# Delta rule on raw keys and queries, with the next head's products handed out in single matmuls

## The chip, the core and the metric

One core of one Trainium2 chip runs the whole program once. The metric is device microseconds for that run. The program computes two small model blocks in float32; the change touches one of their mixers, the chunked gated delta rule with 8 heads.

## The reference, cut to what matters

```python
qkv = silu(causal_depthwise_conv(h @ w_in[qkv]))          # 4 taps, 512 tokens
q = l2norm(q) * 128 ** -0.5                               # l2norm(x) = x * rsqrt(sum(x * x) + EPS)
k = l2norm(k)
beta, g = sigmoid(b_in), -exp(a_log) * softplus(a_in + dt_bias)
# per head, chunks of C tokens, g_cum = cumsum(g) in the chunk, decay = exp(g_cum_i - g_cum_j), j <= i
kb = k * beta
L = where(strict, (kb @ k.T) * decay, 0);  A = L + I
u, w = solve(A, v * beta), solve(A, kb * exp(g_cum))
attn = (q @ k.T) * decay
for each chunk:                                           # state S is 128 x 128
    v_new = u - w @ S
    o = (q * exp(g_cum)) @ S + attn @ v_new
    S = S * exp(g_last) + (k * exp(g_last - g_cum)).T @ v_new
y = (rmsnorm(o, norm_g) * silu(gate)) @ w_out             # rmsnorm divides by sqrt(mean(o * o) + EPS)
```

## The kernel before, in words

Activations lie transposed: channels on 128 partitions, 512 tokens along a row. A head is one tile of 128 channels; its tokens are handled as TT = 4 chunks of 128, each with two blocks of 64 for the triangular inverse. The program is written out engine by engine; each engine runs its own list in order and waits on semaphores.

**Dense products.** TensorE computes the four projections of a head (key, query, value, gate: "slabs" j = 0 to 3) from weights split into a high and a low part, 8 slices of 128 rows by 3 matmuls of 512 columns each: 24 matmuls per slab, 96 per head (lines L618 to L620). They are for head i + 1 and are put between the small products of head i by `fill(first, end)`, in groups of one slice (3 matmuls) to two slices and more. GpSimd splits each slab with two instructions (`split`, L555 high part, L557 low part, both read and write SBUF). `split(s)` waits for `slab_done` of slab s - 3, so a slab's last matmul starts the split of the third slab after it.

**Small products of head i on TensorE,** in order: keys by keys-times-beta into B3 (L911, wait `kb`), keys by queries into B4 (L919, wait `qn`), transposes of the keys into B7 (L643), a transposition of the first inverse (L892, wait `xt`), five levels of the inverse (L892: a group into banks 0 and 1 that waits for `x`, then after a fill two groups `xq` and `xp`), two last steps (L943, L949), w (L957), and for each chunk L964 (u), L968 (minus w by state, waits for `s`), L971 (state by queries), a fill, L975 (state update) and L976 (output). Then `head_squares` (L824: two matmuls by ones, for the squared norms of keys and queries), `head_rows` (L833: decay and beta rows broadcast over partitions), and L983, a matmul by ones of the squared output.

**VectorE** runs the convolution taps of head i + 1 (L2215), the masks and subtractions of the inverse (L2299, L2304, L2308), the state (L2331, L2334), scaled copies of transposed keys and values (`kv_scaled`, L2272), and at the end of a head `ada_rows(i)` (three products with a reduction of 128x1024, L2000, for another part of the program) and `head_start(i + 1)` (L2224 to L2232). The next head begins with L2248 (B3 times decay), four masked copies L2253 and L2256, which releases `xt`. `head_end` (L2237, L2239) makes the gated output of the head before.

**ScalarE** holds the activations, among them `head_rnorms` (log and exp of the norms over 128x512), the exponent of the decay, table loads (Silu set, Ln/Exp set), and copies of PSUM banks.

Of the kernel before, what the change touches and what calls it, by code (L numbers as in the profile page):

```python
# [24 lines left out]
P = 128  # L25
# [137 lines left out]
def build(nc, a, out):  # L163
    ctx = ExitStack()
    with ctx:
# [33 lines left out]
        vraw, osq, ors, head_out = yt[:], A[:, 11], A[:, 10], A[:, 11]  # L199
# [29 lines left out]
        S = sb("S", [P, 2, P])  # L229
        mx, nm, esum, rinv = sb("mx", [P, 2]), sb("nm", [P, 2]), sb("esum", [P, 2]), sb("rinv", [P, 2])  # L230
# [57 lines left out]
        def r_slab(i, j):  # L288
# [25 lines left out]
        tr_ready, pt_ready, pv_done = sem("tr_ready"), sem("pt_ready"), sem("pv_done")  # L314
# [13 lines left out]
            "ab_in", "ab_hi", "ab_lo", "ab_ps", "abT", "ab", "gates", "gsum", "pick", "rowhi", "rowlo", "row", "silu", "sq", "ss", "rn", "rows", "kb", "qn", "dec", "erow", "gram", "ktr",  # L328
# [18 lines left out]
        def half_block(t, tile, b):  # L347

            return t[HALF * b:HALF * b + HALF, tile * HALF:(tile + 1) * HALF]

# [230 lines left out]
        def _(pe):  # L581

            pe.sem_inc(tr_ready, 2)
            pe.sem_inc(pv_done, 2)
# [226 lines left out]
            q, k_, v, gs0, E, dec, gs1, LT, kdec, XT, ktok, wT, Pm, vn = (A[:, n] for n in range(14))  # L811
            gs, attn = (gs0, gs1), dec

            def head_sums(i, chunks):

                for pair in range(2):
                    pair_chunks(SLAB0["gdn"] + i * 4 + 2 * pair, USE0["gdn"] // 2 + i * 2 + pair,
                                [c - 2 * KD * pair for c in chunks if c // (2 * KD) == pair])
# [7 lines left out]
            def head_rows(i):  # L826

                if i:
                    pe.wait_ge(g["s"], i * 3)
                else:  # L830
                    pe.wait_ge(g["rowlo"], 2)
                for n, bank in enumerate((SS, B5)):
                    mm = pe.matmul(bank[:], pick[0:64, i:i + 1].broadcast_to((64, P)), gate_row[:, n, :], start=True, stop=True)  # L833
                mm.then_inc(g["rows"], 1)

            def out_step(name, n, k, ready):

                s, u = SLAB0[name], USE0[name] // 2
                if n == 0:
# [4 lines left out]
                for j in range(2):  # L844
# [28 lines left out]

            def head(i, ahead):

                def fill(first, end, step=None, kv=None, third=()):
                    if ahead:
                        head_sums(i + 1, range(first, end))
                    elif kv is not None:
                        kv_slabs(f"kv{kv // 2}", (kv % 2,))  # L880
                    elif step is not None:
                        out_step("gdn_out", step, step, step + 1)
                    if not ahead:
                        for k in third:
                            out_third("gdn_out", k, k, k + 1)

                def blocks(out, lhs, left, rhs, right, take, put, bs=(0, 1)):

                    for t in range(TT):
                        for b in bs:  # L890
                            at = b ^ (t % 2 & take)
                            mm = pe.matmul(out(t, b ^ (t % 2 & put)), left(lhs, t, at), right(rhs, t, at), start=True, stop=True)  # L892
                    return mm

                def first_two(t, b):
                    return pair_block(0, t, b)

                def next_two(t, b):
                    return pair_block(2, t, b)

                def last_one(t, b):
                    return half_block(B5, t, b)

                def on_ident(rhs, t, b):
                    return rhs[HALF * b:HALF * b + HALF, HALF * b:HALF * b + HALF]

                fill(0, 5, kv=0)
# [5 lines left out]
                fill(5, 7, kv=1)  # L913
                pe.wait_ge(g["qn"], i + 1)
# [6 lines left out]
                turn_over(B7, [k_[:, t * P:(t + 1) * P] for t in range(TT)]).then_inc(g["ktr"], 1)  # L921
                fill(7, 8, kv=2)
# [4 lines left out]
                fill(8, 10, kv=3)  # L927
                for n in range(1, 6):
                    pe.wait_ge(g["x"], i * 6 + n)
                    blocks(first_two, LT, own_block, Xs, half_block, 0, 1).then_inc(g["p_ps"], 1)  # L930
                    fill(8 + 2 * n, 10 + 2 * n, n - 1)
                    if n == 1 and i:
                        pe.wait_ge(yt_ready, i)
# [4 lines left out]
                    if n == 2:  # L938
                        turn_over(B7, [vraw[:, t * P:(t + 1) * P] for t in range(TT)]).then_inc(g["vtr"], 1)

# [4 lines left out]
                fill(20, 22, 5)  # L945
# [5 lines left out]
                fill(22, 24)  # L951

                pe.wait_ge(g["tok"], i + 1)
# [5 lines left out]

                pe.wait_ge(g["v"], i + 1)  # L960
                pe.wait_ge(g["qd"], i + 1)
                for t in range(TT):
                    c = slice(t * P, (t + 1) * P)
                    mm = pe.matmul(B4[:, c], XT[:, c], v[:, c], start=True, stop=t == 0)  # L964
# [7 lines left out]
                    fill(24 + t, 25 + t)  # L972
# [4 lines left out]
                mm.then_inc(g["o_ps"], 1)  # L977
                if ahead:
                    head_squares(i + 1)
                    head_rows(i + 1)  # L980
                fill(28, 30, third=(0, 1))
                pe.wait_ge(g["osq"], i + 1)
                pe.matmul(B4[:], ones, osq, start=True, stop=True).then_inc(g["oss"], 1)  # L983
                fill(30, 32, 6, third=(2, 3, 4))

            head_sums(0, range(KD, KD + 2))
            gates_of_tokens()
            head_sums(0, range(KD + 2, 2 * KD + 3))
            gate_sums()
            head_sums(0, range(2 * KD + 3, 4 * KD))  # L990
            head_squares(0)
            head_rows(0)
# [3 lines left out]
            out_step("gdn_out", 7, 7, 8)  # L996
            for k in range(5, KD):
                out_third("gdn_out", k, k, k + 1)
            out_rest("gdn_out")
# [429 lines left out]
        def _(act):  # L1429
# [181 lines left out]
            q, k_, v, gs0, E, dec, gs1, LT, kdec, XT, ktok, wT, Pm, vn = (A[:, n] for n in range(14))  # L1611
            gs, attn = (gs0, gs1), dec

            def head_sum(i, j):
# [3 lines left out]
                if i:  # L1618
                    act.wait_ge(*((g["ktr"], i), (g["qd"], i), (g["vtr"], i))[j])
# [7 lines left out]
            def head_square(i, j):  # L1627

                act.wait_ge(g["silu"], i * 3 + j + 1)
                act.activation(sq[:, j, :], (k_, q)[j], ACT.Square).then_inc(g["sq"], 1)  # L1630

            def head_rnorms(i):

                for j, (bank, times) in enumerate(((B3, 1.0), (B7, P ** -0.5))):
                    inv_sqrt(g["ss"], i * 2 + j + 1, tb[:, j, :], bank[:], 1.0, times, load=False).then_inc(g["rn"], 1)

            def head_gate(i):

                copy_sum(1, SLAB0["gdn"] + i * 4 + 3, gs[i % 2])

            def head_start(i):

                head_rnorms(i)
                act.wait_ge(g["dec"], i + 1)
                act.activation(dec, dec, ACT.Exp).then_inc(g["edec"], 1)
                act.activation(E, SS[:], ACT.Exp).then_inc(g["erow"], 1)

            def head_end(i):
                inv_sqrt(g["oss"], i + 1, ors, B4[:], 1.0 / P, load=False).then_inc(g["ors"], 1)
                if i == 6:  # L1650

                    act.wait_ge(g["qn"], 8)
                    kv_copies(0)
                act.wait_ge(yt_ready, i + 1)
                high_y(i, i, head_out)

            def head(i, ahead):
                if ahead:
                    head_sum(i + 1, 0)
                    head_sum(i + 1, 1)  # L1660
                act.preload_act_table_set(SILU)
                if not ahead:
                    kv_copies(1)
                act.wait_ge(taken[1], USE0["gdn"] // 2 + i * 2 + 3)
                act.activation(gs[i % 2], gs[i % 2], ACT.Silu).then_inc(g["gs"], 1)
                if ahead:
                    head_silu(i + 1, 0)
                act.wait_ge(g["wt_ps"], i + 1)
                act.activation(wT, B3[:], ACT.Copy, scale=-1.0).then_inc(g["wt"], 1)
                for t in range(TT):  # L1670
# [3 lines left out]
                    if ahead:  # L1674
# [3 lines left out]
                        elif t == 1:  # L1678
# [1120 lines left out]
```

## Time and profile before

| | |
|---|---|
| median of 3 runs | 2233.44 us (2232.42 to 2235.02) |
| profiled execution, first to last instruction | 2231.0 us |
| TensorE busy | 2160.1 us, 97% |
| VectorE, ScalarE, GpSimd busy | 1170.1, 574.0, 1215.7 us |
| mean granted TensorE clock | 0.994 of full speed |

The profiled execution stands 2.4 us under the median, which also counts what lies around the instructions. A busy share tells that an engine had work in flight. What limits a stretch is read from the timeline of each engine: which instruction starts late, and what released it. The delta rule takes the stretch from about 94 us to 469 us.

### The profile page before, as it was taken

Reading aid. Unit: us, or ns where it says so; the run is one execution under the profiler, and the core shown is the slowest. Engines: PE = TensorE matmul, PEld = TensorE weight load, DVE = VectorE, ACT = ScalarE, POOL = GpSimd, SP = SyncE. Lnnn points to the kernel's source line nnn. Section 1 sums busy time; section 2 is a strip of 40 time slices with the busy share of each in tenths; the row PEclk is TensorE's granted clock in tenths of the full one; section 3 lists DMA queues with packets and bytes.
Section 4 is the critical chain, followed back from the end, with each engine's and each line's share of the span. In section 5 each row is a group of like instructions: output and inputs, shape, how many; then the busy total and the mean of one; then the engine's idle time right before and its main releaser. Section 6 shows DMA issues by size and latency. Waiting matters only on the chain.

```text
span 2231.0 us, 29287 instructions
## 1 busy us (share of the span) xinstructions
PE 2160.1 (97%) x11992; PEld 1724.0 (77%) x11992; DVE 1170.1 (52%) x1651; ACT 574.0 (26%) x1043; POOL 1215.7 (54%) x687
## 2 busy tenths in 40 slices
PE   7899999999999999999999999999999999999998
PEld 6677777778888887677788888777777778887886
DVE  4666666658648275554431322467765365346332
ACT  4333423223112022342320201422232230002113
POOL 5433233357868676433566666654436276656663
PEclk9999999999999999999999999999999999999999
DMA  8522322236556453211333333322224133333331
GB/s 271 181 68 80 101 67 86 86 103 206 164 180 198 152 188 109 68 51 39 113 97 101 96 94 96 100 79 67 66 57 128 43 110 98 95 95 94 105 104 66
DMA packets 366018, 239.88 MB, mean 108 GB/s; under 512 B 11351, under 2 KB 350653, under 8 KB 365758
## 3 DMA queue, kind: packets, MB, share of 16 engines
q1 hardware_dynamic: 364268, 234.07, 35.0%
q10 hardware_dynamic: 1618, 3.94, 0.5%
q8 instruction: 96, 1.57, 0.3%
q14 instruction: 36, 0.29, 0.0%
HBM read 233.79 MB, written 4.19 MB: 107 GB/s over the span
## 4 chain that ended last, share of the span: by engine, by line
PE 88%; DVE 6%; ACT 2%; issue 1%; POOL 1%; DMA 1%; SPq 0%; DVEq 0%; ACTq 0%; POOLq 0%
PE bank L599 16%; PE bank L601 16%; PE bank L600 16%; PE bank L618 6%; PE bank L620 5%; PE bank L619 5%; PE mid L892 2%; PE mid L1355 1%; PE bank L635 1%; PE bank L637 1%; PE bank L636 1%; PE bank L846 1%; POOL wL L557 1%; PE mid L643 1%; PE bank L848 1%
## 5 line engine op out<-in xcount | busy, mean ns | idle before, releaser
L555 POOL TENSOR_SCALAR wH<-stage 128x1024 fp32r<-128x1024 f32 (+1 forms) x340 | 386.0, 1135 | 960.1 <-PE bank L620 370.6
L557 POOL TENSOR_TENSOR wL<-stage,wH 128x1024 fp32r<-128x1024 f32 (+1 forms) x340 | 830.5, 2443 | 28.4
L599 PE MATMUL bank<-hH,wH 128*128 128x512 f32 x944 | 368.6, 390 | 0.7 <-DVE A L2077 0.3
L601 PE MATMUL bank<-hH,wL 128*128 128x512 f32 x944 | 367.4, 389 | 0.0
L600 PE MATMUL bank<-hL,wH 128*128 128x512 f32 x944 | 367.3, 389 | 0.0
L599 PE MATMUL bank<-RA,wH 128*128 128x512 f32 (+1 forms) x788 | 283.9, 360 | 5.5 <-DVE RA L2091 3.0
L601 PE MATMUL bank<-RA,wL 128*128 128x512 f32 (+1 forms) x788 | 281.7, 358 | 0.0
L600 PE MATMUL bank<-RA,wH 128*128 128x512 f32 (+1 forms) x788 | 281.6, 357 | 0.0
L618 PE MATMUL bank<-hH,wH 128*128 128x512 f32 x544 | 239.4, 440 | 6.5 <-POOL wL L557 6.2
L620 PE MATMUL bank<-hH,wL 128*128 128x512 f32 x544 | 214.1, 394 | 0.0
L619 PE MATMUL bank<-hL,wH 128*128 128x512 f32 x544 | 213.4, 392 | 0.0
L599 PEld LDWEIGHTS bank<-hH,wH 128*128 128x128 f32 x944 | 177.2, 188 | 39.8 <-issue 3.3
L600 PEld LDWEIGHTS bank<-hL,wH 128*128 128x128 f32 x944 | 177.2, 188 | 36.8 <-issue 0.2
L601 PEld LDWEIGHTS bank<-hH,wL 128*128 128x128 f32 x944 | 177.2, 188 | 36.8
L599 PEld LDWEIGHTS bank<-RA,wH 128*128 128x128 f32 x788 | 149.3, 189 | 29.5 <-DVE RA L2091 3.2
L600 PEld LDWEIGHTS bank<-RA,wH 128*128 128x128 f32 x788 | 149.4, 190 | 21.6 <-issue 0.5
L601 PEld LDWEIGHTS bank<-RA,wL 128*128 128x128 f32 x788 | 149.3, 190 | 21.4
L1508 ACT ACTIVATE A<-bank 128x512 f32<-128x512 f32 (+1 forms) x85 | 47.2, 558 | 384.1 <-PE bank L601 354.6
L2000 DVE CUSTOM_DVE_ANT_0 WIDE<-WIDE,cbc,vec 128x1024 f32<-128x1024 f32 x80 | 142.9, 1831 | 0.1
L2060 DVE SCALAR_TENSOR_TENSOR xT<-bank,modT,xT 128x512 f32<-128x512 f32 x62 | 46.4, 750 | 172.8 <-PE bank L601 164.6
L2129 DVE TENSOR_TENSOR A<-bank,A 128x512 f32<-128x512 f32 x44 | 30.5, 692 | 197.4 <-PE bank L601 191.8
L618 PEld LDWEIGHTS bank<-hH,wH 128*128 128x128 f32 x544 | 102.6, 189 | 39.3 <-issue 12.6
(406 smaller groups left out, 3232.7 us busy)
## 6 DMA issues: line engine op xcount, KB each, us to landing
WIDE<-in_ada_t SPq DMA_DIRECT2D x46, 1024.0 KB, 6.0
stage<-in_ffn_w_gate SPq DMA_DIRECT2D x44, 512.0 KB, 3.8
stage<-in_ffn_w_up SPq DMA_DIRECT2D x44, 512.0 KB, 3.8
stage<-in_c_wkv SPq DMA_DIRECT2D x32, 512.0 KB, 3.9
stage<-in_gdn_w_in SPq DMA_DIRECT2D x32, 512.0 KB, 4.0
stage<-in_ffn_w_down SPq DMA_DIRECT2D x32, 512.0 KB, 3.8
stage<-in_o_w_in SPq DMA_DIRECT2D x32, 512.0 KB, 4.0
stage<-in_e_w_in SPq DMA_DIRECT2D x26, 512.0 KB, 3.7
```

Source lines behind the costliest of these rows:

```text
L555: pool.tensor_scalar(high[:, 0:n], raw[:, 0:n], 1.0, 0.0, ALU.mult, ALU.add).then_inc(w_high, 1)
L557: pool.tensor_tensor(low[:, 0:n], raw[:, 0:n], high[:, 0:n].bitcast(F32), ALU.subtract).then_inc(w_split, 1)
L599: pe.matmul(bank[:, 0:n], h[:, k, c], xh[:, k, :], start=first and k == 0, stop=False)
L600: pe.matmul(bank[:, 0:n], h[:, k, c], xl[:, k, :], start=False, stop=False)
L601: mm = pe.matmul(bank[:, 0:n], l[:, k, c], xh[:, k, :], start=False, stop=last and k == kc - 1)
L618: pe.matmul(acc[j % 2][:], h, hH[:, k, :], start=k == 0, stop=False)
L619: pe.matmul(acc[j % 2][:], h, hL[:, k, :], start=False, stop=False)
L620: mm = pe.matmul(acc[j % 2][:], l, hH[:, k, :], start=False, stop=k == KD - 1)
L892: mm = pe.matmul(out(t, b ^ (t % 2 & put)), left(lhs, t, at), right(rhs, t, at), start=True, stop=True)
L1508: act.activation(out, acc[b][:, 0:n], func).then_inc(taken[b], 1)
L2000: ins = dve.tensor_tensor_reduce(out=w, in0=w, in1=c_bank if n < ADA_HEAD else cbc[:], scale=1.0, scalar=vec[:, at:at + 1], op0=ALU.mult, ...
L2060: dve.scalar_tensor_tensor(out=xT[:, k, :], in0=bank[:], scalar=gate[:, k:k + 1], in1=xT[:, k, :], op0=ALU.mult, op1=ALU.add).then_inc(tak ...
```

## The change

Keys and queries are no longer normalised over 128x512. The norm of a key becomes a factor per token, taken from squares of the transposed keys (`key_squares`, sums over 128x128 tiles into `k_sum`) and put into the bias of the decay's exponent, into `kdec_by` and into `v_by`. The norm of the query goes into the output norm (`head_sums`). The two matmuls by ones of L824 and the mask `strict` are gone; scaled copies move from VectorE to ScalarE in four tiles each; the dense products are counted in single matmuls (`head_units`) and spread in more and smaller groups. Cut to its core:

```diff
-        vraw, osq, ors, head_out = yt[:], A[:, 11], A[:, 10], A[:, 11]
+        vraw, osq, ors, head_out = yt[:], A[:, 17], A[:, 16], A[:, 17]
...
@@ TensorE
-            def head_squares(i):
-                for j, bank in enumerate((B3, B7)):
-                    pe.wait_ge(g["sq"], i * 2 + j + 1)
-                    pe.matmul(bank[:], ones, sq[:, j, :], start=True, stop=True).then_inc(g["ss"], 1)
+            def head_squares(i):
+                pe.wait_ge(g["osum"], i + 1)
+                pe.matmul(B4[:], ones, osq, start=True, stop=True).then_inc(g["oss"], 1)
...
-                fill(0, 5, kv=0)
+                at = dense(9)
+                if not ahead:
+                    kv_slabs("kv0", (0,))
+                if i:
+                    head_squares(i - 1)
+                at = dense(3)
                 pe.wait_ge(g["kb"], i + 1)
...
-                fill(5, 7, kv=1)
-                pe.wait_ge(g["qn"], i + 1)
+                at = dense(9)
...
-                turn_over(B7, [k_[:, t * P:(t + 1) * P] for t in range(TT)]).then_inc(g["ktr"], 1)
-                fill(7, 8, kv=2)
+                at = dense(3)
                 pe.wait_ge(g["xt"], i * 7 + 1)
...
-                fill(8, 10, kv=3)
+                at = dense(6)
                 for n in range(1, 6):
                     pe.wait_ge(g["x"], i * 6 + n)
                     blocks(first_two, LT, own_block, Xs, half_block, 0, 1).then_inc(g["p_ps"], 1)
-                    fill(8 + 2 * n, 10 + 2 * n, n - 1)
+                    at = dense(3)
...
                     blocks(last_one, Ps, half_block, XTs, half_block, 1, 1).then_inc(g["xp"], 1)
+                    at = dense(3)
...
-                fill(20, 22, 5)
+                at = dense(3)
...
-                fill(22, 24)
+                at = dense(6)
...
                 for t in range(TT):
+                    elif ahead:
+                        keys_turn(i + 1)
-                    fill(24 + t, 25 + t)
+                    at = dense(4)
                     pe.wait_ge(g["vn"], i * 4 + t + 1)
...
+                    at = dense(2)
+                    if ahead and t == 1:
+                        head_rows(i + 1, 0)
+                    if ahead and t == TT - 1:
+                        head_rows(i + 1, 1)
+                at = dense(3)
...
@@ ScalarE
+            def head_open(i):
+                if i:
+                    head_squares(i - 1)
+                act.preload_act_table_set(LN_EXP)
+                own.settle()
+                act.activation(k_log, k_sum, ACT.Ln, bias=EPS).then_inc(g["rk"], 1)
+                act.wait_ge(g["rk"], 3 * i + 1)
+                act.activation(k_inv2, k_log, ACT.Exp, scale=-1.0).then_inc(g["rk"], 1)
+                act.activation(k_norm, k_log, ACT.Exp, scale=0.5).then_inc(g["rk"], 1)
+                act.wait_ge(g["dec"], i + 1)
+                act.wait_ge(g["kds"], 3 * i + 1)
+                for t in range(TT):
+                    ins = act.activation(decs[i % 2][:, c], decs[i % 2][:, c], ACT.Exp, bias=dec_bias[:, t:t + 1])
+                ins.then_inc(g["edec"], 1)
...
@@ VectorE
-            def head_start(i):
...
+            def key_factors(i):
+                dve.wait_ge(g["rk"], 3 * i + 1)
+                dve.scalar_tensor_tensor(out=dec_bias, in0=k_log, scalar=-1.0, in1=tok[:, 0, :, i],
+                                         op0=ALU.mult, op1=ALU.subtract).then_inc(g["kds"], 1)
+                dve.wait_ge(g["rk"], 3 * i + 3)
+                dve.tensor_tensor(kdec_by, k_inv2, tok[:, 3, :, i], ALU.mult).then_inc(g["kds"], 1)
+                dve.tensor_tensor(v_by, k_norm, tok[:, 1, :, i], ALU.mult).then_inc(g["kds"], 1)
+            def head_sums(i):
+                dve.wait_ge(g["osq"], i + 1)
+                dve.wait_ge(g["sq"], i + 1)
+                dve.scalar_tensor_tensor(out=osq, in0=sq[:, i % 2, :], scalar=Q_EPS, in1=osq,
+                                         op0=ALU.mult, op1=ALU.add).then_inc(g["osum"], 1)
...
-                ada_rows(i)
-                if ahead:
-                    head_start(i + 1)
+                if ahead:
+                    decay_rows(i + 1)
+                    keys_by_beta(i + 1)
+                head_sums(i)
+                if ahead:
+                    key_factors(i + 1)
+                ada_rows(i)
```

`decay_rows` adds the table `decay_neg` to SS (PSUM) in one 128x512 instruction; `keys_by_beta` multiplies B5 (PSUM) by the keys. The gated output of head i - 1 (`head_scaled`, `head_gated`) now reads a copy `vn` of B6 that ScalarE makes. `between(n)` of VectorE now holds at n = 1 `head_scaled`, n = 2 `head_gated`, n = 3 E times q, n = 4 `low_y`, n = 5 a tap of the query; `below(n)` the key's three taps at n = 1 to 3 and a query tap at n = 4.

## Rows read from the trace of the kernel before

**Rows 1.** Page, busy time of the engines, with share of the span and instructions.
```profile
PE 2160.1 (97%) x11992; PEld 1724.0 (77%) x11992; DVE 1170.1 (52%) x1651; ACT 574.0 (26%) x1043; POOL 1215.7 (54%) x687
```
**Rows 2.** Busy time by stretch: start:end length, PE, PEld, DVE, ACT, POOL, PEclk, DMA share, GB/s.
```profile
270.40:315.60 45.20, 43.80 (x436) 33.12 (x435) 30.21 (x63) 15.46 (x28) 14.04 (x8) 1.00 0.30 94
```
**Rows 3.** Timeline of PE: start, length, line, tiles, count; end of one head, start of next.
```profile
270.43 0.38 PE L976 MATMUL mid<-A 128*128 128x128 f32 x2
270.65 1.02 PE L824 MATMUL mid<-sq,tab 128*128 128x512 f32 x2
...
272.46 0.72 PE L833 MATMUL mid<-RA,pick 64*128 64x512 f32 x2
...
273.45 0.40 PE L619 MATMUL bank<-hL,wH 128*128 128x512 f32 x1
273.69 0.40 PE L620 MATMUL bank<-hH,wL 128*128 128x512 f32 x1
...
284.66 0.46 PE L892 MATMUL mid<-tab,inv 64*64 64x64 f32 x16
```
**Rows 4.** Timeline of PE, one level of the inverse in the same head.
```profile
288.84 0.46 PE L892 MATMUL mid<-A,inv 64*64 64x64 f32 x16
289.12 0.63 PE L892 MATMUL mid<-inv,A 64*64 64x64 f32 x16
289.92 0.46 PE L892 MATMUL mid<-inv,A 64*64 64x64 f32 x16 [0.16 <-DVE inv L2304]
...
290.64 0.40 PE L619 MATMUL bank<-hL,wH 128*128 128x512 f32 x1
```
**Rows 5.** Timeline of PE, last step of the inverse and the chunks of that head.
```profile
305.16 0.68 PE L949 MATMUL mid<-A 64*64 64x64 f32 x8 [0.41 <-DVE A L2319]
...
310.13 0.46 PE L968 MATMUL mid<-S,A 128*128 128x128 f32 x2
...
311.34 0.38 PE L975 MATMUL mid<-A 128*128 128x128 f32 x2
...
312.25 0.46 PE L968 MATMUL mid<-S,A 128*128 128x128 f32 x2
...
315.59 0.38 PE L976 MATMUL mid<-A 128*128 128x128 f32 x2
```
**Rows 6.** Timeline of DVE around the start of that head.
```profile
269.65 1.27 DVE L2000 CUSTOM_DVE_ANT_0 WIDE<-WIDE,cbc,vec 128x1024 f32<-128x1024 f32 x1
...
273.26 1.12 DVE L2224 SCALAR_TENSOR_TENSOR A<-mid,tok,tab 128x128 f32<-128x128 f32 x4
...
281.43 0.69 DVE L2248 TENSOR_TENSOR A<-mid,A 128x512 f32<-128x512 f32 x1 [5.13 <-PE mid L911]
282.16 1.24 DVE L2253 TENSOR_TENSOR inv<-A,tab 64x128 f32<-64x128 f32 x4
283.43 0.42 DVE L2256 TENSOR_TENSOR inv<-tab,inv 128x256 f32<-128x256 f32 x1
...
284.38 0.16 DVE L2259 COPY chunk_decay<-A 128x4 f32<-128x4 f32 x1
```
**Rows 7.** Timeline of ACT, end of that head.
```profile
315.70 1.28 ACT L1684 ACT_TABLE_LOAD   x1
```
**Rows 8.** Timeline of POOL in that head.
```profile
277.18 1.05 POOL L555 TENSOR_SCALAR wH<-stage 128x1024 fp32r<-128x1024 f32 x1 [11.26 <-PE bank L620]
...
284.89 1.05 POOL L555 TENSOR_SCALAR wH<-stage 128x1024 fp32r<-128x1024 f32 x1 [4.19 <-PE bank L620]
```
**Rows 9.** Timeline of DVE in the last head.
```profile
417.47 3.35 DVE L2253 TENSOR_TENSOR inv<-A,tab 64x128 f32<-64x128 f32 x4
...
422.66 2.35 DVE L2259 COPY chunk_decay<-A 128x4 f32<-128x4 f32 x1
```
**Rows 10.** Timeline of POOL in the last head.
```profile
417.65 2.39 POOL L557 TENSOR_TENSOR wL<-stage,wH 128x1024 fp32r<-128x1024 f32 x1
```
**Rows 11.** Timeline of PE in the last head, a wait.
```profile
429.43 0.47 PE L846 MATMUL bank<-RA,wH 128*128 128x512 f32 x1 [1.87 <-ACT tb L1508]
```
**Rows 12.** Busy time by stretch, as in rows 2, shortly after that wait.
```profile
430.20:433.50 3.30, 3.30 (x52) 2.51 (x50) 0.62 (x2) 0.00 (x0) 2.14 (x1) 0.50 0.51 145
```

More of the change, by code:

```diff
@@ L826, in head_rows @@
-            def head_rows(i):
-                if i:
[L829 to L836, printed above, removed]
+            q, k_, v, gs0, E, dec0, gs1, LT, kdec, XT, ktok, wT, Pm, vn = (A[:, n] for n in range(14))
@@ new lines, in _, with head_units @@
+            gs, attns = (gs0, gs1), (dec0, A[:, 14])
+            def head_units(i, first, end):
+                for n in range(first, end):
+                    j, k, part = n // (3 * KD), n // 3 % KD, n % 3
+                    s, uses = SLAB0["gdn"] + i * 4 + j, USE0["gdn"] // 2 + i * 2 + j // 2
+                    if k == 0 and part == 0:
+                        pe.wait_ge(w_split, s + 1)
+                        free(j % 2, uses)
+                    h, l = (w[:, k, :] for w in halves(s))
+                    mm = pe.matmul(acc[j % 2][:], l if part == 2 else h, (hL if part == 1 else hH)[:, k, :],
+                                   start=k == 0 and part == 0, stop=k == KD - 1 and part == 2)
+                    if k == KD - 1 and part == 2:
+                        mm.then_inc(slab_done, 1)
@@ new lines, in head_rows, with keys_turn @@
+            def head_rows(i, n):
+                if i == 0:
+                    pe.wait_ge(g["rowlo"], 2)
+                elif n == 0:
+                    pe.wait_ge(g["p"], i * 6)
+                else:
+                    pe.wait_ge(g["s"], i * 3)
+                pe.matmul((SS, B5)[n][:], pick[0:64, i:i + 1].broadcast_to((64, P)), gate_row[:, n, :],
+                          start=True, stop=True).then_inc(g["rows"], 1)
+            def keys_turn(i):
+                pe.wait_ge(g["silu"], i * 3 + 1)
+                if i:
+                    pe.wait_ge(g["v"], i)
+                turn_over(B7, [k_[:, t * P:(t + 1) * P] for t in range(TT)]).then_inc(g["ktr"], 1)
@@ L843, in out_step @@
                 pe.wait_ge(y_ready, ready)
-                for j in range(2):
+                for j in js:
                     h, l = (w[:, k, :] for w in halves(s + j))
@@ L872, in out_rest, with blocks, first_two, next_two @@
                             behind(k)
+            def blocks(out, lhs, left, rhs, right, take, put, bs=(0, 1)):
+                for t in range(TT):
+                    for b in bs:
+                        at = b ^ (t % 2 & take)
+                        mm = pe.matmul(out(t, b ^ (t % 2 & put)), left(lhs, t, at), right(rhs, t, at), start=True, stop=True)
+                return mm
+            def first_two(t, b):
+                return pair_block(0, t, b)
+            def next_two(t, b):
+                return pair_block(2, t, b)
@@ L877, in fill @@
                     if ahead:
[L878 to L893, printed above, removed]
@@ L2386, in _ @@
             conv(0, 2, (2, 1, 0))
-            head_start(0)
+            decay_rows(0)
+            keys_by_beta(0)
+            key_factors(0)
             for i in range(0, 7):
```

282 lines of the change are left out of this document (147 added, 135 removed).

## The prediction

> **What bounds the kernel now.** I read the engines' busy time first: TensorE is busy 97% of the span [rows 1], so a change counts only by what it does to TensorE's list. Next, the table by stretch over one head: TensorE has 43.80 us of work in 45.20, at the full clock (1.00, that is 2.4 GHz), VectorE 30.21, GpSimd 14.04 in 8 instructions [rows 2]. Seven heads repeat this. I call T the start of the last chunk's output product L976; T is 270.43 for one head and 315.59 for the next, so a head takes 45.16 us [rows 3, 5]. Then the timelines of TensorE, VectorE and GpSimd side by side: who would be late if TensorE came sooner? In the kernel before nobody is: VectorE's three long products run from T - 0.8 to T + 2.8, GpSimd's splits start at T + 6.8 and T + 14.5, and VectorE, which waited 5.13 us, starts L2248 at T + 11.0 [rows 6, 8]. That order is what the change moves.
>
> **TensorE's own list, per head.** Dense matmuls start 0.23 apart [rows 3].
> - Gone: the two matmuls by ones, from 270.65 to 272.46: -1.8 [rows 3].
> - Chunks: from a state update L975 to the next use of the state L968 it is 0.91 us [rows 5], while three products lie between at 0.22 each (L976 takes 0.22 to the next start [rows 3]): 0.25 is waiting, thrice. Two dense matmuls now stand there and hide it: -0.75, and at most as much again because the first product after a wait starts cold; I take -1.0.
> - Before L949 0.41 of waiting [rows 5] is covered by the dense group that follows more closely: -0.4.
> - Levels of the inverse: from the second group after a fill (289.12) to the next level's first (289.92) it takes 0.80, of which some 0.35 waits for VectorE [rows 4]: the first group of 16 needed 0.28, and this one is 0.17 longer (0.63 against 0.46). Three dense matmuls now stand in that gap. But a group of 64x64 products costs to enter and to leave: from 289.92 to the second dense matmul at 290.64 it takes 0.72, 0.2 more than 0.28 + 0.23 [rows 4]; entering costs another 0.1. So 0.35 is won and 0.3 paid, five times: -0.3, between -1.8 (the switch is free) and +1.5 (the wait stays).
> - The row products (L833) are split over two places, one more switch: +0.3, between 0 and 0.6. The key transposes only move.
> Sum: -1.8 - 1.0 - 0.4 - 0.3 + 0.3 = -3.2; the smaller waits at the first transposition and the first chunk bring it to -3.6. If nothing else were late a head would take 41.6.
>
> By the Trainium skill, "TensorEngine Tiling (Array Packing)", changing the tiling mode drains TensorE. The 0.2 and 0.1 above agree with it; it speaks against the smaller groups, and without it the levels would give -1.8 instead of -0.3.
>
> **Work that moves to ScalarE** (tile copies, squares of 128x128) lies beside 45 us of TensorE work with 15.46 busy [rows 2]; I cost it at nothing, at most 0.5 a head where a copy sits behind another. No row shows a square with a sum; the chunk copies are its neighbours.
>
> **Where VectorE now comes late.** TensorE reaches the wait for `xt` sooner: before at T + 14.2 (284.66) with 36 dense matmuls in between [rows 3]; now 29 (2, 12, 3, 9, 3), without the ones products, one row product and the key transposes: 14.2 - 1.6 - 1.8 - 0.3 - 0.45 = about 10.2. But VectorE's three L2000 (269.65 to 273.26, 3.6 us [rows 6]) now stand behind `keys_by_beta`, `head_sums` and `key_factors`. `keys_by_beta` waits for the second row product, issued after the last chunk, so it runs from T + 1.4 to 2.0; `head_sums` to T + 2.7. `key_factors` waits for a logarithm that stands behind a table load of 1.28 [rows 7], after the squared output that waits for L976: T + 2.6. That would still do: 2.7 + 0.2 + 3.6 = 6.5, then L2248 0.73, L2253 1.27, L2256 0.4: `xt` at T + 9.
>
> The splits break it. The gate slab of the next head is now finished three matmuls after the second row product: its split starts at T + 2.4 instead of T + 6.8 [rows 8]; the key slab's at T + 10.5 instead of T + 14.5. In the last head, L2253 was caught by a split: four small products took 3.35 us instead of 1.24, from 417.47, while L557 ran from 417.65 for 2.39 [rows 6, 9, 10]. The first product went through, GpSimd came in, and the other three stood until it ended. A copy of 128x4 was held too, 2.35 instead of 0.16 [rows 6, 9]. So the two engines take turns, one instruction each. In turns from T: `head_sums` to 2.7; L555, 1.05 [rows 8], to 3.7; the first small factor to 3.9; L557 to 6.3; two more factors to 6.4; L2000 thrice to 10.0; L2248 to 10.7; but L555 of the next split came in at 10.5 and holds to 11.6; first L2253 to 11.9; L557 to 14.3; three more L2253 to 15.25; L2256 to 15.7. TensorE has waited from 10.2 to 15.7: +5.5. Bounds: +2.2 if only the first split is in the chain (2.0 + all VectorE work of 7.0 + 3.5 = 12.5), +5.9 if the first factor also misses its turn. A pure 5.5 - 3.6 is +1.9 a head.
>
> By the Trainium skill, "SBUF — State Buffer", section "Who interferes with whom", VectorE with two inputs in SBUF and a GpSimd instruction that reads SBUF exclude each other for a whole instruction, and one with an input in PSUM isn't held. The first half is what rows 9 and 10 show. Applied to `head_sums`, whose form these rows don't contain, it says that `head_sums` takes a turn too; the sum holds it as one.
>
> **The clock.** After a wait of 1.87 on TensorE [rows 11] the granted clock was 0.50, its level of 1.2 GHz, from 430.2 to 433.5 [rows 12]. 3.3 us at half speed is 1.6 lost. A wait of 5.5 in every head should bring the same: +1.6, between 0 and 2.2.
>
> **Sum.** A head: -3.6 + 5.5 + 1.6 = +3.5. Six of them: +21. The first head has no L2000 before it and only gains: -1. The last head has the same wait, but also had a slow clock before, and its first products for the output fill old waits: +1. At its end L2000 now starts after the squared output instead of under the chunks, which delays the last head's norm: +1, between 0 and 2. Together +22: 2231.0 becomes 2253, and the median 2233.4 becomes 2255. This case's own range is 2243 to 2266, from +2 to +5 a head.
>
> **Rivals.**
> - *The first split only.* `xt` at T + 12.5, wait 2.2, clock fall 1.6, list -3.6: +0.2 a head. 2233 + 1 + 1 = 2235, between 2226 and 2240. For it: L2253 would have to finish before T + 10.5. Against it: L2000 ends at 10.0 only.
> - *No turns in this place* (the other side: not slower). If VectorE's queued instructions run through and the split waits for a gap, `xt` is there at T + 9 and nobody waits. Place: VectorE between `head_sums` and L2256. It decides from `xt` before T + 10.2. Then -3.6 a head, -22 for six, -1, -6 in the last, +1: 2206, between 2198 and 2218. Against it: the single L2253 that went through in [rows 9].
> - *A third collision.* `low_y` at level 4 of the inverse reads two tiles of SBUF, and the value slab's predecessor is finished just then; if it comes after L557 has started, it holds back the level by up to 2.4, of which 0.7 is slack: +1.7 a head, 2267, up to 2275.
> - *The handing out does nothing:* the waits at levels and chunks stay. Then +1.8 a head on top of the forecast: also about 2267.
>
> **How the numbers follow.** Forecast 0.58, first split only 0.14, no turns 0.16, the last two together 0.12. Predicted 2255. To leave out no more than 0.2 (no turns, and the far ends), the range runs from 2226 to 2270. A measurement of this kernel can tell 0.2%, 4.5 us, from no change. Faster by more (under 2229): no turns and the lower part of first split, 0.21. Same: 0.11. Slower (over 2238): 0.68.
>
> **What would show it.** The table by stretch: a head of about 48.7, PEclk under 1.00 in it, GpSimd and VectorE longer in instructions that did not change (L2253 over 3 us, L557 or L555 over their 2.39 and 1.05). TensorE's waits: the L892 released by L2256 with some 5 us, seven times. No L824, waits before L968 and L949 gone, levels still 3.0 apart. Wrong would be: that wait absent or near 2, splits that start elsewhere than T + 2.4 and T + 10.5, or new waits for ScalarE.

## The result, and the profile of the changed kernel

| | before | changed |
|---|---|---|
| median | 2234.07 us (2232.42 to 2235.02, 4 runs) | 2257.68 us (2256.59 to 2259.46, 4 runs) |
| ratio, 95% interval | | 1.0104 [1.0092, 1.0117] |
| profiled span | 2231.0 | 2254.8 |
| mean granted clock | 0.994 | 0.987 |

The change costs 23.6 us. The page shows hardly any of it; TensorE, VectorE and GpSimd did as much as before [rows 1], TensorE in a longer span:

```profile
PE 2159.7 (96%) x11960; PEld 1721.9 (76%) x11960; DVE 1173.2 (52%) x1595; ACT 604.2 (27%) x1234; POOL 1216.9 (54%) x687
```

One head by stretch, as in [rows 2] (length, PE, PEld, DVE, ACT, POOL, PEclk, DMA share, GB/s), and under it pieces of three heads behind the new wait:

```profile
278.40:326.20 47.80, 43.39 (x431) 32.78 (x430) 31.71 (x55) 19.25 (x52) 14.18 (x8) 0.96 0.29 89
293.10:296.10 3.00, 2.98 (x22) 2.34 (x22) 0.63 (x2) 0.96 (x2) 0.00 (x0) 0.50 0.98 264
341.00:347.20 6.20, 6.20 (x59) 4.18 (x61) 1.65 (x3) 0.96 (x2) 0.00 (x0) 0.50 0.32 88
390.20:395.00 4.80, 4.78 (x40) 3.41 (x41) 1.08 (x4) 0.96 (x2) 0.00 (x0) 0.50 0.62 161
```

TensorE has fewer instructions than in [rows 2] (431 for 436) and takes 2.6 us longer over them, with 4.4 us idle where it had 1.4. T is again the start of the last chunk's output product, now L1023. Before, the last eight T are 135.12, 180.07, 225.26, 270.43, 315.59, 361.09, 406.29 and 456.80; now 134.51, 182.52, 230.51, 278.40, 326.23, 375.51, 424.12 and 478.49. So: -0.6 in the first head, +18.4 over the six in the middle (48.27 a head for 45.19), +3.9 in the last (54.37 for 50.51), +2.1 behind it. Sum +23.8, the difference of the spans.

What TensorE waited for from 130 to 500 us (who waited, for whom: total, times, longest):

```profile
PE mid L898 <- DVE inv L2348: 26.1, 6, 4.4
PE bank L865 <- POOL wL L567: 6.0, 1, 6.0
PE bank L865 <- DVE RA L2162: 4.6, 1, 4.6
```

The first line is the wait for `xt`. Here it is in one head (T = 278.40), with VectorE and GpSimd beside it, in this order; they answer [rows 3], [rows 6] and [rows 8]:

```profile
293.12 0.71 PE L898 MATMUL mid<-tab,inv 64*64 64x64 f32 x16 [4.35 <-DVE inv L2348]
```
```profile
280.32 0.68 DVE L2317 SCALAR_TENSOR_TENSOR A<-sq,A 128x512 f32<-128x512 f32 x1
280.97 0.96 DVE L2307 SCALAR_TENSOR_TENSOR kn<-kn,tok 128x4 f32<-128x4 f32 x1
281.85 0.16 DVE L2310 TENSOR_TENSOR kn<-kn,tok 128x4 f32<-128x4 f32 x1
...
282.00 3.47 DVE L2080 CUSTOM_DVE_ANT_0 WIDE<-WIDE,cbc,vec 128x1024 f32<-128x1024 f32 x1
...
288.52 4.08 DVE L2345 TENSOR_TENSOR inv<-A,tab 64x128 f32<-64x128 f32 x4
292.64 0.42 DVE L2348 TENSOR_TENSOR inv<-tab,inv 128x256 f32<-128x256 f32 x1
```
```profile
280.74 1.18 POOL L565 TENSOR_SCALAR wH<-stage 128x1024 fp32r<-128x1024 f32 x1 [6.87 <-PE bank L832]
282.00 2.39 POOL L567 TENSOR_TENSOR wL<-stage,wH 128x1024 fp32r<-128x1024 f32 x1
288.93 1.10 POOL L565 TENSOR_SCALAR wH<-stage 128x1024 fp32r<-128x1024 f32 x1 [4.55 <-PE bank L832]
290.12 2.34 POOL L567 TENSOR_TENSOR wL<-stage,wH 128x1024 fp32r<-128x1024 f32 x1
```

Read across: a factor of 128x4 takes 0.96 instead of 0.16 beside the split's first instruction, an ada product 3.47 instead of 1.28 beside the second, the masked copies 4.08 instead of 1.24 [rows 6] beside the next split. The splits start at T + 2.3 and T + 10.5, `xt` is there at T + 14.7, and TensorE would have come at T + 10.4.

In the last head, two more things are late (SyncE's queue, GpSimd, TensorE):

```profile
433.20 0.37 SPq L381 DMA_DIRECT2D WIDE<-in_ada_t  x1
433.99 18.86 SPq L372 DMA_DIRECT2D stage<-in_gdn_w_out  x5
```
```profile
441.41 1.05 POOL L565 TENSOR_SCALAR wH<-stage 128x1024 fp32r<-128x1024 f32 x1 [6.00 <-DMA stage<-in_gdn_w_out]
```
```profile
448.82 0.80 PE L865 MATMUL bank<-RA,wH 128*128 128x512 f32 x1 [6.01 <-POOL wL L567]
```

The ada load waits for VectorE's second product of head 6 (it ends at 433.1), and the output weights stand behind it in the queue; the two then come in side by side, with the DMA engines busy 0.86 of the time from 433.2 to 441.4 (before, between the weights' load and their split, 0.43).

### The profile page after: what moved, and what is told of

The parts are those of the page before. It is cut to its first block, busy times and chain, and to the rows that moved or that the text cites. A ratio compares the mean times of both kernels' runs of the same rounds, so it can differ in the third digit from the quotient of the medians.

```text
span 2254.8 us, 29386 instructions
## 1 busy us (share of the span) xinstructions
PE 2159.7 (96%) x11960; PEld 1721.9 (76%) x11960; DVE 1173.2 (52%) x1595; ACT 604.2 (27%) x1234; POOL 1216.9 (54%) x687
## 4 chain that ended last, share of the span: by engine, by line
PE 86%; DVE 7%; POOL 2%; ACT 2%; DMA 1%; issue 1%; SPq 1%; ACTq 0%; DVEq 0%; POOLq 0%
PE bank L608 15%; PE bank L610 15%; PE bank L609 15%; PE bank L832 7%; PE bank L627 3%; PE bank L629 3%; PE bank L628 3%; PE mid L898 2%; DVE WIDE L2080 2%; POOL wL L567 1%; PE mid L1406 1%; PE bank L644 1%; PE bank L646 1%; PE bank L645 1%; PE bank L865 1%
## 5 line engine op out<-in xcount | busy, mean ns | idle before, releaser
L608 PE MATMUL bank<-hH,wH 128*128 128x512 f32 x944 | 368.5, 390 | 0.7 <-DVE A L2157 0.3
L610 PE MATMUL bank<-hH,wL 128*128 128x512 f32 x944 | 367.4, 389 | 0.0
L609 PE MATMUL bank<-hL,wH 128*128 128x512 f32 x944 | 367.3, 389 | 0.0
L608 PE MATMUL bank<-RA,wH 128*128 128x512 f32 (+1 forms) x788 | 284.0, 360 | 6.7 <-DVE RA L2171 3.0
L608 PEld LDWEIGHTS bank<-hH,wH 128*128 128x128 f32 x944 | 177.2, 188 | 39.8 <-issue 3.2
L608 PEld LDWEIGHTS bank<-RA,wH 128*128 128x128 f32 x788 | 149.6, 190 | 30.9 <-issue 3.7
L2080 DVE CUSTOM_DVE_ANT_0 WIDE<-WIDE,cbc,vec 128x1024 f32<-128x1024 f32 x80 | 163.5, 2087 | 0.9 <-DMA WIDE<-in_ada_t 0.8
L627 PE MATMUL bank<-hH,wH 128*128 128x512 f32 x296 | 128.6, 434 | 6.6 <-POOL wL L567 6.4
L832 PE MATMUL bank<-hH,wH 128*128 128x512 f32 x248 | 117.4, 473 | 0.5
L629 PE MATMUL bank<-hH,wL 128*128 128x512 f32 x296 | 116.5, 393 | 0.0
L628 PE MATMUL bank<-hL,wH 128*128 128x512 f32 x296 | 116.1, 392 | 0.0
```

Source lines behind the costliest of these rows:

```text
L608: pe.matmul(bank[:, 0:n], h[:, k, c], xh[:, k, :], start=first and k == 0, stop=False)
L609: pe.matmul(bank[:, 0:n], h[:, k, c], xl[:, k, :], start=False, stop=False)
L610: mm = pe.matmul(bank[:, 0:n], l[:, k, c], xh[:, k, :], start=False, stop=last and k == kc - 1)
L627: pe.matmul(acc[j % 2][:], h, hH[:, k, :], start=k == 0, stop=False)
L628: pe.matmul(acc[j % 2][:], h, hL[:, k, :], start=False, stop=False)
L629: mm = pe.matmul(acc[j % 2][:], l, hH[:, k, :], start=False, stop=k == KD - 1)
```

## The experiments

My theory: two-operand work of VectorE and GpSimd's splits take turns; `xt` queues behind both splits and the three ada products; the wait and the low clock behind it are the loss. The rivals are that one split, or the products' place, or the clock, or the list of matmuls explains it. In the kernels of 2, 3 and 10, which have three lines more near the top, a line number is 3 higher than in the changed kernel (L901 for L898, L2351 for L2348).

**1. The ada products moved to idle places.**

```diff
                 if ahead:
                     conv(i + 1, 1, (0,))
+                ada_rows(i, (0, 1))
                 for t in range(TT - 1):
...
                         conv(i + 1, 2, (2 - t,))
+                    if t == 1:
+                        ada_rows(i, (2,))
...
                     key_factors(i + 1)
-                ada_rows(i)
```

> Changed kernel, with the three ada products of a head (L2080) taken from the head's end, between the three small key factors and the L times decay product, to places in the same head where VectorE waits for the state loop: two ahead of the first state copy, one behind the second state update. Nothing is added or left out. Theory (VectorE's products of two SBUF operands and GpSimd's splits take turns, and the inverse's start xt queues behind both splits and all three ada products): without the products the four masked copies end at T+8.7, before the second split starts at T+10.5; xt at T+9.1, TensorE wants it at T+10.4, so the 4.35 us wait goes and with it the low clock (1.3 to 2.9 us); a head falls from 47.9 to about 42.2 us, 34 to 36 us over six heads. In the last head the ada products no longer end late, so SyncE's queue no longer holds the output weights behind an ada load: 6 to 8 us more. 2257.7 - 42 = about 2215 us (2208 to 2224), faster than the kernel before. Rival A (it is the splits alone: xt would be late without the products too): xt still 2 us or more late, 2235 or above. Rival B (the list of matmuls itself is longer than I take it, 44 or more a head without any wait): above 2226 with no wait of TensorE for xt.

Measured: 2213.33 us (2212.59 to 2215.18), 0.9906 [0.9891, 0.9921] of the kernel before. It is faster than both kernels. The head periods are 42.10 to 42.16 us, the last head 46.52. One head, then `xt`, then what stands ahead of it:

```profile
261.20:303.20 42.00, 41.93 (x431) 31.76 (x430) 27.13 (x55) 19.21 (x52) 14.14 (x8) 1.00 0.32 101
```
```profile
271.42 0.46 PE L898 MATMUL mid<-tab,inv 64*64 64x64 f32 x16
```
```profile
268.66 1.24 DVE L2345 TENSOR_TENSOR inv<-A,tab 64x128 f32<-64x128 f32 x4
269.93 0.42 DVE L2348 TENSOR_TENSOR inv<-tab,inv 128x256 f32<-128x256 f32 x1
```

The same 431 matmuls and 55 instructions of VectorE; TensorE idles 0.07 us, and VectorE has 4.6 us less "work", which was being held. `xt` at T + 9.2, the wait gone, and in the last head the wait for the output weights too. Rivals A and B of this run fall.

**2 and 3. The splits moved instead.** VectorE's order is untouched; GpSimd gets a wait (`r % 4 == 3` where only the second split is meant).

```diff
+                r = s - SLAB0["gdn"]
+                if 6 <= r < 32 and r % 4 in (2, 3):
+                    pool.wait_ge(g["xt"], 7 * (r // 4 - 1) + 1)
                 pool.wait_ge(w_loaded[s % 2], (s // 2 + 1) * 16)
```

> Changed kernel with one more wait on GpSimd: the splits of slabs 2 and 3 of the next head start only when xt of this head is ready (they now run at T+2.3 and T+10.5). VectorE's order is untouched, the ada products stay where they are. Theory (turns): each ada product takes 1.28 instead of up to 3.47 us, the masked copies 4 x 0.31 instead of 4.08; xt at T+9.1, no wait of TensorE for it; both splits then run T+9 to T+16, beside the first levels, where two or three VectorE products of two SBUF operands are held instead. A head 42.2 to 43 us, the last head as it is in the changed kernel: 2257.7 - 6 x 5.3 = about 2225 us (2220 to 2232). Rival A (the place of the products alone counts, not the splits): xt still about 4 us late, 2250 or above. Rival B (held operations beside the levels cost what is saved): xt without a wait but levels over 4 us apart, 2240 or above.

> Changed kernel, with only the second of the two splits (slab 3, now at T+10.5) made to wait for xt; the first (slab 2, T+2.3) stays. It prices the two collisions apart. Theory (turns with each split): the first ada product still takes about 3.5 us, the four masked copies run free (4 x 0.31 in place of 4.08), xt at about T+11.8 instead of T+14.7; TensorE waits about 1.4 us for it. Per head 2.9 us less, and more where so short a wait doesn't bring the clock down (1.3 to 1.6 us): 2257.7 - 6 x 2.9 to 6 x 4.5 = 2231 to 2240 us. Rival A (the masked copies are slow for another reason than the split): no change, 2254 or above. Rival B (the first split holds nothing that matters): xt at T+9.5 as with both splits moved, about 2225.

Measured: both splits behind `xt` 2220.09 us, 0.9934 [0.9918, 0.9951], a head 42.11 us; only the second 2229.40 us, 0.998 [0.9971, 0.9989], a head 43.70. In the latter the first collision stands, the second is gone, and the wait is 1.5 us with the clock at 1.00 behind it:

```profile
268.08 3.46 DVE L2083 CUSTOM_DVE_ANT_0 WIDE<-WIDE,cbc,vec 128x1024 f32<-128x1024 f32 x1
...
274.60 1.24 DVE L2348 TENSOR_TENSOR inv<-A,tab 64x128 f32<-64x128 f32 x4
```
```profile
276.36 0.46 PE L901 MATMUL mid<-tab,inv 64*64 64x64 f32 x16 [1.53 <-DVE inv L2351]
```
```profile
276.30:279.30 3.00, 2.94 (x40) 2.18 (x41) 1.03 (x5) 0.96 (x2) 2.83 (x2) 1.00 1.03 389
```

So each collision has its price: the first puts `xt` 2.7 us later (T + 9.1 to T + 11.8), the second 2.9 more (to T + 14.7). With either engine out of the way the head is the same 42.1: neither the products nor the splits are slow for a reason of their own. The last head stays at 54.2 and 54.4 in these two, with its wait of 5.8 and 6.0 for the output weights: that is a separate loss.

**4. The wait filled with work.**

```diff
+                if ahead:
+                    s1 = SLAB0["gdn"] + (i + 1) * 4 + 1
+                    pe.wait_ge(w_split, s1 + 1)
+                    if i:
+                        pe.wait_ge(g["oc"], i)
+                    for _ in range(14):
+                        pe.matmul(B6[:], halves(s1)[0][:, 0, :], hH[:, 0, :], start=True, stop=True)
                 pe.wait_ge(g["xt"], i * 7 + 1)
```

> Changed kernel with 14 needless matmuls of 128x512 (0.233 us apart, 3.3 us in all) ahead of TensorE's wait for xt in each head but the last, into a bank that is overwritten later. Nothing else differs, the wait for xt stays. It prices the low clock alone: VectorE's chain is as late as it was, but TensorE works through most of the wait. Theory (the low clock behind the wait costs 1.3 to 2.9 us a head): xt still at T+14.7, a wait of about 1.1 us, the dense group behind it at 0.23 instead of 0.42 us apart; six heads by 1.3 to 2.0: 2245 to 2250 us. Rival (what is done at the low clock is hidden behind VectorE and ScalarE in any case): within 3 us of the changed kernel's 2257.7.

Measured: 2249.90 us (2249.42 to 2253.93), 7.8 less than the changed kernel with 98 matmuls more. A head takes 46.57 us: 42.10, 14 times 0.233, and a wait of 1.20. Nothing is left for the clock, and it was 1.00 behind the wait:

```profile
292.50:295.50 3.00, 2.99 (x41) 2.18 (x41) 1.04 (x4) 0.96 (x2) 0.00 (x0) 1.00 0.98 264
```

The rival falls: the low clock is a loss of its own. In the changed kernel the six heads took 289.6 us; less six times 42.10 and the 26.1 of waiting, 10.9 are left, 1.8 a head (1.4 to 1.6 in four, 2.8 and 2.1 in two).

**5. The products in their old place,** ahead of the next head's decay rows:

```diff
+                ada_rows(i)
                 if ahead:
                     decay_rows(i + 1)
...
                     key_factors(i + 1)
-                ada_rows(i)
```

> Changed kernel with the three ada products put back where the kernel before has them: ahead of the next head's decay rows, not between the key factors and the L times decay product. Theory (turns): they run from T-1.2 to about T+3.5, the last of them held by the split at T+2.3; the sum for the output norm (L2317, two SBUF operands) is then held by that split too and ends near T+6.7, where TensorE wants it at T+4.1: a wait of about 2.6 us at the squares product. The masked copies come before the second split (which itself moves behind), xt near T+11 is no longer waited for. A head 42.1 + 2.6 = 44.7 us, 3.2 less than in the changed kernel; the last head some 4 to 6 us less, since the ada products end earlier. 2257.7 - 19 - 5 = about 2233 us (2227 to 2241): as fast as the kernel before, and slower than with the products moved early. Rival (the place just behind the key factors is no worse than any other, all collisions only move along): xt or the squares still waited for by 4 us or more a head, 2250 or above.

Measured: 2235.57 us, 1.0011 [1.0002, 1.002], heads of 44.6. The sum for the norm is held instead, for 2.09 us more than its 0.68, and the squares wait (VectorE; GpSimd; TensorE; two heads):

```profile
273.37 2.77 DVE L2317 SCALAR_TENSOR_TENSOR A<-sq,A 128x512 f32<-128x512 f32 x1
```
```profile
273.25 2.35 POOL L567 TENSOR_TENSOR wL<-stage,wH 128x1024 fp32r<-128x1024 f32 x1
```
```profile
276.20 1.12 PE L919 MATMUL mid<-A,tab 128*128 128x512 f32 x2 [2.26 <-DVE A L2317]
365.37 1.12 PE L919 MATMUL mid<-A,tab 128*128 128x512 f32 x2 [2.23 <-DVE A L2317]
```
```profile
276.00:279.00 3.00, 2.80 (x15) 2.15 (x16) 0.37 (x4) 2.68 (x7) 0.00 (x0) 1.00 0.87 258
366.00:369.00 3.00, 3.00 (x14) 2.59 (x13) 0.00 (x0) 2.97 (x8) 0.00 (x0) 0.63 0.63 171
```

So the reordering cost the changed kernel some 22 us against the old order (2257.68 less 2235.57), and the old order still 22 against a good one. The last two lines are stretches behind two waits of one length: the clock stayed at 1.00 in one and fell in the other (that head took 46.2). In the four other heads, behind waits of 2.23 to 2.26, it stayed at 1.00.

**6. The same move in the kernel before** (same diff as in 1).

> The kernel before (not the changed one), with its three ada products moved to the same idle places of VectorE: two ahead of the first state copy, one behind the second state update. It asks whether the move is a gain by itself or only takes away what the change brought. Theory: in the kernel before TensorE never waits for what stands behind the products, and the splits meet none of them; a head stays at 45.1 to 45.3 us, the time within 2 us of 2233.6. Rival (the products at a head's end cost the kernel before something too, say through the start of the next head's chain): 2229 or less.

Measured: 2234.96 us, 1.0002 [0.9992, 1.0011]; a head 45.2. The move is no gain by itself, it takes away what the change brought. So the change on its own, with its chain kept short, is worth 21 us.

**7 to 9. The terms of the list,** each put back into the kernel of experiment 1, where TensorE has no waits.

Levels (then nothing behind the second group):

```diff
-                    at = dense(3)
+                    at = dense(6)
```

Chunks (`dense(3)` at the head's end becomes `dense(15)`):

```diff
-                    at = dense(4)
+                    at = dense(3)
...
-                    at = dense(2)
```

Ones:

```diff
                 pe.wait_ge(g["osum"], i + 1)
+                for _ in range(2):
+                    pe.matmul(B4[:], ones, osq, start=True, stop=True)
```

> Kernel with the products early (2213.3 us, no waits in the list), in which the five levels of the inverse are handed out as in the kernel before: all six dense matmuls of a level between its first and its second group of small ones, none behind the second, in place of three and three. The levels are 3.1 to 3.4 us apart now. Prediction's own figure: the grouping is worth 0.3 us a head between a gain of 1.8 and a loss of 1.5. At 0.3 a head, seven heads: 2215.4 us. At the end of no effect: 2213; at the far end 2226. Rival (fewer changes between the array's modes pay for the waits): 2208 or less.

> Kernel with the products early (2213.3 us), in which the four chunks of a head get their dense matmuls as in the kernel before: three ahead of each wait for ScalarE's copy and none behind, and the twelve that are left in one piece at the head's end. Now they get four ahead and two behind, and show no wait. Prediction's own figure: the chunks' waits, 1.0 us a head; seven heads: 2213.3 + 7 = about 2220 us (2217 to 2223), with waits of TensorE for the copy of vn back in the trace. Rival (the waits only move elsewhere, the state's chain being covered by less than it seems): within 2 us of 2213.

> Kernel with the products early (2213.3 us), with two further fp32 products of the ones with the squared output per head (into the same bank, ahead of the one that counts): as many ones products as the change removed. It prices that term of the prediction. Theory: the two stand in a list without waits and cost their full 0.90 us each, 1.8 a head; eight heads of them, seven inside the head periods and one at the end: 2213.3 + 14 = about 2227 us (2225 to 2229), a head 43.9. Rival (part of a product is hidden by the weights' loads or by waits that follow): 2222 or less.

Measured: levels 2219.64 us (head 42.89), chunks 2216.96 (42.60), ones 2228.24 (43.80), against 2213.33 (42.10). A ones product costs 0.85 of the 0.90 a row gives it, 1.70 a head. The chunks are worth 0.50 a head, half of what I said, and just under the range that I gave for that run; the trace names no wait of TensorE for the copy of `vn`, only the products by the state (L1011) start later in two of three chunks (0.41 and 0.47 behind L1007, where they stood 0.22 behind). The levels' 0.8 is nearly all another thing: with six dense matmuls in one piece, TensorE reaches a slab's first product before VectorE has taken the last slab's bank (L2286, the convolution tap that reads it). That wait of 0.73 taken off, the five levels take 15.64 us (276.11 to 292.48), as they do in two groups of three.

```profile
286.83 0.47 PE L832 MATMUL bank<-hH,wH 128*128 128x512 f32 x1 [0.73 <-DVE A L2286]
```

**10. The queue in the last head.** In the changed kernel, the ada load goes behind two tiles of the output weights:

```diff
-            head_ada(7)
-            residual_loads("gdn_out", a["gdn_w_out"][0], KD)
+            for i in range(KD):
+                if i == 2:
+                    head_ada(7)
+                load(SLAB0["gdn_out"] + i, v[i], KD)
```

> Changed kernel in which SyncE's queue loads the last ada tile behind the first two tiles of the output weights, not ahead of all of them. Everything else is as in the changed kernel, its waits for xt too. Theory (in the last head that load waits for VectorE's last ada products of head 6, and the output weights queue behind it, so that GpSimd splits them late and TensorE waits 6.0 us at the first output product, with a low clock behind): the 6 us wait goes, the last head falls from 54.4 to 47 to 49 us: 2250 to 2252 us. Rival (the output weights are late for GpSimd's or the DMA queues' own reasons): the wait stays, 2256 to 2258.

Measured: 2255.31 us (2254.79 to 2256.84), the last head 54.23. The wait for the output weights is gone, as the theory says, but the time is not the 2250 to 2252 that it gave, and lies just under the rival's 2256: the output splits, which began at T + 11.3 instead of T + 17.3, ran into the masked copies of the last head, and TensorE waited for `xt` there instead.

```profile
435.66 6.33 DVE L2348 TENSOR_TENSOR inv<-A,tab 64x128 f32<-64x128 f32 x4
```
```profile
442.51 0.70 PE L901 MATMUL mid<-tab,inv 64*64 64x64 f32 x16 [5.16 <-DVE inv L2351]
```

Both have to be cured together, which the products moved early do (46.52 us).

## Why the prediction came out as it did

The sign, the size and the main mechanism were right: forecast 2255, measured 2257.7. By its steps:

- **The list** was to fall by 3.6 a head; it fell by 3.06 (45.16 to 42.10). Right: TensorE reaches the wait for `xt` at T + 10.4 (forecast 10.2, though the terms written there add up to 10.05), the ones products (1.70 for 1.8), the wait before L949. Wrong in size: the chunks (0.50 for 1.0; the 0.25 that I added for a cold first product isn't there, nor a third of the 0.75 of waiting), and the levels. From the first group of the first level to the last step (L943, now L983) it took 15.63 us before, 286.87 to 302.50, and takes 15.63 in the kernel of experiment 1, 273.40 to 289.03: 0.0 for the -0.3 forecast. No wait is left in them, so the changes between 64x64 and 128x128 products seem to take all that the waits gave; that is read from these rows and from experiment 7, and no run prices one change by itself. The "smaller waits" that made 3.6 out of 3.2 were a guess. The terms that were measured (1.70, 0.50, 0.4 before L949, 0.0) make 2.6 of the 3.06; where the rest comes from no run shows.
- **Splits and turns.** They start at T + 2.3 and T + 10.5 (forecast 2.4 and 10.5), L2307, L2080 and L2345 are held. `xt` came at T + 14.7, not 15.7. The turns weren't one instruction each: behind the split's first instruction all three small factors went through, not one, and GpSimd's second began only beside the first ada product (282.00 for both), so that this product took the hold, and the other two ran at 1.28. So the masked copies began sooner than I had them, and two of the four (0.28 each) had begun before the second split came at 288.93; the third was held by its first instruction (1.01), the fourth by its second (2.40), where I had three still to run behind it. The wait was 4.35, not 5.5.
- **The clock** fell as said; 1.8 a head on average for 1.6, and experiment 4 makes it a cost of its own. Two size errors, a wait too long by 1.15 and a list too short by 0.5, cancelled in part; six heads gave +18.4 for +21. That 2255 came so near to 2257.7 is partly luck: what the six heads fell short of the forecast (2.6), the last head made up (2.9) by a wait that I hadn't seen.
- **Rivals.** *First split only*: its condition didn't hold, since the masked copies began at T + 10.1 and two of them met the second split; experiment 3 makes it true by hand and shows what it would have given, 1.5 us of waiting without a fall of the clock. *No turns* falls by every held instruction. *A third collision* didn't come: L2162 took 0.95 for 0.68 or so at level 4, within its slack. *Handing out does nothing* falls for the chunks and for L949; for the levels it is as good as true.
- **The last head** was missed: +1 forecast, +3.9 measured. The step that failed said that this head has the same wait for `xt`: `xt` came at T + 14.7 here too, but TensorE's list ahead of it is longer in this head, and it came at the same moment (L898 at 438.89, 0.07 of waiting). What I left out was a queue that the moved products hold up. Before, the ada load left at T + 1.7 (408.01), and the output weights at T + 10.3, as soon as a split freed their buffer. Now the buffer is free at T + 6.0 (430.10), but the ada load stands ahead and leaves at T + 9.1, the weights at T + 9.9, and they land 7.4 later, where 4.0 is their median, with the ada tile coming in beside them. TensorE wants them at T + 18.7 now, where it first took them at T + 23.1 before (429.43 [rows 11]): earlier at one end, not at the other.
- **The end** was to cost +1; behind the last T it cost +2.1, but only 1.2 of this is the change's. Up to the first product of what follows the delta rule it took 12.0 us before (L599 at 468.77) and takes 13.2 now (L608 at 491.68). The other 0.9 falls in the part that both kernels have alike, where the kernel of experiment 6 took 2.3 us more than the kernel before, with one stretch at a granted clock of 0.50 more (about 933 us). Of the 1.2, half is the place of the products: in experiment 1, where none stands there, it is 12.6. The norm's new sum isn't late there: VectorE's next step (L2323) starts at T + 4.3, as L2237 did at T + 4.4 before, and at T + 5.3 in the changed kernel. What is left lies with TensorE: its wait for L2162 is 3.6 us there, where the kernel before had 0.82 at this place, and the products behind it ran at a granted clock of 0.50 (experiment 1, 441 to 444 us):

```profile
441.00:444.00 3.00, 2.79 (x7) 2.21 (x8) 1.07 (x3) 0.26 (x1) 0.98 (x1) 0.50 0.00 0
```

The section of the Trainium skill that I weighed ("SBUF — State Buffer", "Who interferes with whom") held for `head_sums` too: as L2317 in experiment 5 it was held, 2.77 us. That VectorE with an input in PSUM isn't held is shown where the second split was moved (VectorE, then GpSimd beside it): two such instructions keep their 0.68 and 0.42 within the splits, the next, with both inputs in SBUF, takes 1.17, where it takes 0.74 beside no split in the changed kernel (297.36), and ends 0.55 behind the split.

```profile
276.29 0.68 DVE L2355 TENSOR_TENSOR A<-mid,A 128x512 f32<-128x512 f32 x1
278.94 0.42 DVE L2381 TENSOR_TENSOR A<-mid,tab 128x256 f32<-128x256 f32 x1 [1.97 <-PE mid L901]
279.28 1.17 DVE L2326 SCALAR_TENSOR_TENSOR A<-A,vec 128x512 f32<-128x512 f32 x1
```
```profile
276.39 1.05 POOL L568 TENSOR_SCALAR wH<-stage 128x1024 fp32r<-128x1024 f32 x1 [5.93 <-DVE inv L2351]
277.52 2.38 POOL L570 TENSOR_TENSOR wL<-stage,wH 128x1024 fp32r<-128x1024 f32 x1
```

By the Trainium skill, "TensorEngine Tiling (Array Packing)", "Key Properties", a change of tiling mode drains TensorE; the levels agree, with 0.0 where the waits alone would have given -1.8.

## What to carry to other kernels

When TensorE's list is shortened, redo the timeline of the chain that feeds its next wait, including the instructions of no urgency that stand in that chain: here three products that nobody needed, in front of the one thing that TensorE waits for, turned a gain of 21 us into a loss of 24. Put such work where the engine already waits, clear of GpSimd's instructions that read SBUF where its own operands both lie there, and follow each semaphore it raises into the load queues. An instruction whose time differs between heads with the same operands may be held: compare its row with the other engine's at the same moment before costing it.

## What the runs showed of the hardware

- A held instruction is charged whole: 0.96 for a 128x4 factor of 0.16, 3.47 for a product of 1.28, 6.33 for four copies of 0.31 each. Counting busy time, VectorE seemed to work 31.71 us in a head, where the same 55 instructions took 27.13 in experiment 1.
- The clock stayed at 1.00 behind idle times of 1.20 and 1.53 us (in the runs of 3 and 4, whose heads are all of one length), fell behind one of 2.23 and not behind five others of 2.23 to 2.26 in the same run, and fell behind each of the six of 4.35, for 3.0 us at least and in one head for 6.2 or more; in the kernel before it fell behind 1.87 [rows 11, 12]. The length of the idle time alone doesn't say which.
